# Branch projections as three-pass split products, and first inputs of four row-wise products split beside the stage ahead of them

## The reference

```
merged = gm[:, :, 0] * (o_nsa @ w_br_nsa[i]) + gm[:, :, 1] * (o_mla @ w_br_mla[i])
x = x + _rmsnorm(merged @ w_o[i], g_post_mix[i])
h = _rmsnorm(x, g_pre_ffn[i])
u = _causal_dwconv(h @ w_up[i], w_conv[i], b_conv[i])
a, v = u[..., :D_FF], u[..., D_FF:]
x = x + _rmsnorm((jax.nn.gelu(a) * v) @ w_down[i], g_post_ffn[i])
```

## Time and profile before

| | |
|---|---|
| median of 3 runs | 2354.74 us (2350.78 to 2355.29) |
| the profiled execution | 2355.66 us, span 2353.9 us |
| PE, DVE, ACT, POOL busy | 93%, 45%, 34%, 10% of the span |
| granted TensorE clock, mean | 0.95 |
| moved by DMA | 191.94 MB, 82 GB/s |

### The profile page before, as it was taken

The page is one execution under the profiler, slowest core; times in us unless marked ns, Lnnn a source line. Parts: engine busy times, 40 slices in busy tenths (PEclk is TensorE's granted clock), DMA queues, the critical chain, the costliest instruction groups (busy, mean ns, idle before and its releaser), DMA issues. The chain is left out here.

```text
span 2353.9 us, 26016 instructions
## 1 busy us (share of the span) xinstructions
PE 2178.9 (93%) x10269; PEld 1754.1 (75%) x10269; DVE 1048.0 (45%) x1829; ACT 808.5 (34%) x1467; POOL 227.4 (10%) x347
## 2 busy tenths in 40 slices
PE   6999989899999997999886899999999878999998
PEld 5886554678887874888775788788778657887887
DVE  4333662455554344222885433333442555333333
ACT  3154660343333233322012332322341664223222
POOL 8100000100000002000552100000110011000000
PEclk9999999999999998999676899999999988999999
DMA  5336311233332221322000133223243102232231
GB/s 133 86 107 96 44 36 54 89 99 90 107 91 90 96 101 45 107 90 90 18 1 1 63 107 97 100 90 100 80 134 125 54 1 75 96 108 90 90 108 72
DMA packets 162103, 191.94 MB, mean 82 GB/s; under 512 B 22866, under 2 KB 133757, under 8 KB 161981
## 3 DMA queue, kind: packets, MB, share of 16 engines
q1 hardware_dynamic: 157536, 176.15, 23.7%
q0 software_dynamic: 3904, 13.97, 3.2%
q10 hardware_dynamic: 541, 0.15, 0.0%
HBM read 182.91 MB, written 7.34 MB: 81 GB/s over the span
## 5 line engine op out<-in xcount | busy, mean ns | idle before, releaser
L1259 DVE TENSOR_TENSOR WHL<-raw,WHL 128x1024 fp32r<-128x1024 f32 x312 | 382.3, 1226 | 732.8 <-ACT WHL L808 732.6
L808 ACT ACTIVATE WHL<-raw 128x1024 fp32r<-128x1024 f32 x312 | 328.3, 1053 | 624.7 <-PE bank L1961 414.1
L1961 PE MATMUL bank<-WHL,HXh 128*128 128x512 f32 x1888 | 512.5, 394 | 18.1 <-DVE HXl L1267 12.3
L1860 PE MATMUL bank<-HXh,WHL 128*128 128x512 f32 x1248 | 494.6, 396 | 5.0 <-DVE BIG L1383 1.8
L1862 PE MATMUL bank<-HXh,WHL 128*128 128x512 f32 x1248 | 489.2, 392 | 0.0
L1961 PEld LDWEIGHTS bank<-WHL,HXh 128*128 128x128 f32 x1888 | 358.5, 190 | 95.8 <-issue 19.3
L1861 PE MATMUL bank<-HXl,WHL 128*128 128x512 f32 x1056 | 413.6, 392 | 0.0
L1860 PEld LDWEIGHTS bank<-HXh,WHL 128*128 128x128 f32 x1248 | 237.3, 190 | 55.2 <-issue 5.7
L1862 PEld LDWEIGHTS bank<-HXh,WHL 128*128 128x128 f32 x1248 | 236.9, 190 | 49.9
L1961 PE MATMUL bank<-WHL,HXl 128*128 128x512 f32 x880 | 273.2, 392 | 0.0
L1861 PEld LDWEIGHTS bank<-HXl,WHL 128*128 128x128 f32 x1056 | 200.3, 190 | 40.5
(11 more groups left out here) (292 smaller groups left out, 2521.0 us busy)
## 6 DMA issues: line engine op xcount, KB each, us to landing
raw<-in_mlp_w_up_dram SPq DMA_DIRECT2D x64, 512.0 KB, 4.6
raw<-in_mlp_w_down_dram SPq DMA_DIRECT2D x64, 512.0 KB, 4.3
raw<-in_w_up_dram SPq DMA_DIRECT2D x44, 512.0 KB, 4.9
raw<-in_a_w_in_dram SPq DMA_DIRECT2D x32, 512.0 KB, 4.3
raw<-in_w_in_dram SPq DMA_DIRECT2D x24, 512.0 KB, 4.8
raw<-in_w_down_dram SPq DMA_DIRECT2D x22, 512.0 KB, 4.1
raw<-in_w_kv_dram SPq DMA_DIRECT2D x16, 512.0 KB, 4.7
rel_dram<-GB POOLq DMA_DIRECT2D x1, 5120.0 KB, 54.5
```

Source lines behind the costliest of these rows:

```text
L808: return a.activation(dst, src, ACT.Copy, **k)
L1259: v.tensor_tensor(dst(1), src, dst(0).bitcast(F32), ALU.subtract).then_inc(w_lo, 1)
L1860: m.matmul(b[:, :], w[0][:, k, :], x[0][:, k, :], start=(k == 0), stop=False)
L1961: ins = m.matmul(bank[2 * tt + h][:, :], x, w[:, h * HALF:(h + 1) * HALF], start=(k == 0 and i == 0), stop=(k == nk - 1 and i == 2))
```

## The change

1. The branch weights are no longer in WHOLE: each slot is two units, split by ACT and DVE like other weights. The inputs are split too: high copies from HT to HX2l on ACT (`branch_high`), low parts in place of HT, as HXh, on DVE (`branch_low`). PE makes 24 split products a unit (`branch_product`), in eight banks, over b = 0 to 3 (half and branch) and j = 0, 1 (which two of the four k).
2. The first four inputs of w_o, down, down0 and down1 (EARLY) get tensors of their own, HX2h and HXl for w_o and HX2h alone for the others (`row_x`), and are split inside the stage ahead: on ACT by `rows_begin`, on DVE by `rows_split` with begin, which then returns. The stage's own call makes the rest.
3. The output of every row-wise product starts at bank 4 (`ybank`), so tiles 0 and 1 lie in banks 4 to 7. PE's wait for the whole stage ahead becomes one ahead of tile 2 at k = 0; for w_o the tiles go 2, 3, 0, 1 at k = 0, with a wait each.

The core of the diff:

```diff
-WHOLE = ("nsa_ck_w1", "nsa_cv_w1", "w_uq", "w_ukv", "br_nsa", "br_mla", "ple")
+WHOLE = ("nsa_ck_w1", "nsa_cv_w1", "w_uq", "w_ukv", "ple")
+EARLY = ("w_o", "down", "down0", "down1")
...
+        def ybank(tt, h):
+            return bank[(2 * tt + h + 4) % 8]
@@ ACT, attention_pairs @@
+                    if p == P_ALL:
+                        branch_high(0)
                     if p + 1 < p1:
                         exp_pair(p + 1)
...
+                    if p == P_ALL:
+                        split(branch_unit(0))
@@ ACT, after the attention @@
+            split(branch_unit(0, 1))
+            branch_high(4)
+            split(branch_unit(1))
+            for b in range(4):
+                split(branch_unit(b) + HL)
+                split(branch_unit(b) + HL + 1)
+                if b == 2:
+                    rows_begin(mergedT, "w_o", lambda k: (merged, k + 1))
             act.wait_ge(ps_full, GT["br"][0] + 16)
-            split(unit_at["w_o", 0])
@@ DVE, the loop over 16 groups @@
+                if f4 == 0:
+                    split(branch_unit(i // 4) + HL)
...
+                if f4 == 3:
+                    split(branch_unit(i // 4) + HL + 1)
+                if i == 11:
+                    rows_split("w_o", mergedT)
+            rows_split("w_o", mergedT, False)
@@ DVE, the up stage, after its waits for the group and for conv_act @@
+                    if j == NFF - 1 and s == 1:
+                        rows_split("down", uT)
@@ DVE, mlp, ahead of its wait for the relu @@
+                    if f == NFF2 - 1:
+                        rows_split(f"down{l}", uT)
@@ PE, split_rows @@
+                    if k == 0 and name == "w_o":
+                        pe.wait_ge(ps_free["vec"], GT["br"][2] + (14, 16, 10, 12)[tt])
+                    elif k == 0 and tt == 2 and name in EARLY:
+                        up = {"down": "up", "down0": "up0", "down1": "up1"}[name]
+                        pe.wait_ge(ps_free[GT[up][1]], GT[up][2] + (2 * NFF if up == "up" else NFF2))
@@ PE, branch_product @@
+                        m.matmul(dst[:, :], wh[:, k, cols_], HX2l[:, n, :], start=(j + k == 0), stop=False)
+                        m.matmul(dst[:, :], wh[:, k, cols_], HXh[:, n, :], start=False, stop=False)
+                        ins = m.matmul(dst[:, :], wl[:, k, cols_], HX2l[:, n, :], start=False, stop=(j == 1 and k == 1))
...
-            pe.wait_ge(merged, KD)
+            for b in range(4):
+                for j in range(2):
+                    branch_product(b, j)
```

More of the change, by code:

```diff
@@ L537, in ht0, with row_x @@
             return 8 * n
+        def ybank(tt, h):
+            return bank[(2 * tt + h + 4) % 8]
+        def row_x(name, k):
+            if name == "w_o" and k < 4:
+                return HX2h[:, k, :], HXl[:, k, :]
+            if name in EARLY and k < 4:
+                return HX2h[:, k, :], HX2h[:, 4 + k, :]
+            h, l = pair(name == "w_o")
+            return h[:, k % KD, :], l[:, k % KD, :]
         def pair(first_block):
@@ L831, in high @@
                         act.wait_ge(*unit_free[w + k - KD])
[L832 to L837, removed]
+                    copy(row_x(name, k)[0], x[:, k, :]).then_inc(x_hi, 1)
+                if name in EARLY:
+                    split(w + 2)
+                else:
+                    for k in range(4):
+                        high(k)
+                        if k == 1:
+                            split(w + 2)
                 for k in range(nk):
@@ L842, in rows_split, with rows_begin @@
                         split(w + k + HL)
+            def rows_begin(x, name, ready):
+                for k in range(4):
+                    act.wait_ge(*ready(k))
+                    copy(row_x(name, k)[0], x[:, k, :]).then_inc(x_hi, 1)
             def wait_group(name, i):
@@ L939, in turned_pair, with branch_high @@
                         copy(probT(p, x)[:, 512 * i:512 * (i + 1)], bank[4 + i][:, :]).then_inc(pt_act, 1)
+            def branch_high(k0):
+                for k in range(k0, k0 + 4):
+                    act.wait_ge(o_evac, k + 1)
+                    copy(HX2l[:, k, :], HT[:, k, :]).then_inc(br_hi, 1)
             def attention_pairs(p0, p1, per):
@@ L1076, in _ @@
                         split(unit_at["up", 2 * j + s] + HL)
+                    if j == NFF - 1 and s == 0:
+                        rows_begin(uT, "down", lambda k: (u_ready, k + 1))
                 act.wait_ge(conv_vec, 2 * j + 1)
@@ L1266, in low @@
                     vec.wait_ge(x_hi, x0[name] + k + 1)
[L1267 to L1273, removed]
+                    xh, xl = row_x(name, k)
+                    v.tensor_tensor(xl, x[:, k, :], xh.bitcast(F32), ALU.subtract).then_inc(x_lo, 1)
+                if begin:
+                    for k in range(4):
+                        low(k)
+                        if k == 1 and name not in EARLY:
+                            split(w + 2)
+                    if name in EARLY:
+                        return
+                else:
+                    split(w + 2)
                 for k in range(nk):
@@ L1550, in _, with branch_low @@
             attention_pairs(P_MLA, P_ALL, lambda p: lambda x: caus, lambda p: None)
+            def branch_low(k0):
+                for k in range(k0, k0 + 4):
+                    vec.wait_ge(br_hi, k + 1)
+                    v.tensor_tensor(HXh[:, k, :], HT[:, k, :], HX2l[:, k, :].bitcast(F32),
+                                    ALU.subtract).then_inc(br_lo, 1)
+            branch_low(0)
+            split(branch_unit(0))
+            split(branch_unit(0, 1))
+            branch_low(4)
+            split(branch_unit(1))
             for i in range(16):
@@ L1973, in split_rows @@
                     x_ready_for(k)
-                    for tt in range(TT):
+                    for tt in ((2, 3, 0, 1) if k == 0 and name == "w_o" else range(TT)):
                         ins = products(k, tt, *w)
```

75 lines of the change are left out of this document (43 added, 32 removed).

## The result

The changed kernel takes 2323.52 us in the median, the kernel before 2352.76 in the runs beside it: a ratio of 0.9872 (0.9853 to 0.9892), 30 us faster (25 to 35). The 30 us come from the ratio; the two medians lie 29.2 apart. One of the four executions of the changed kernel took 4337.55 us and is left out of the ratio; it is in the median, which is 2323.08 without it. The forecast was 2329.5, range 2324 to 2338: the direction is right, the time lies half a microsecond outside the range.

What follows compares the result with a forecast made beforehand. TensorE (PE), busy 93% of the span, was taken as the bound. Savings of 18.1 (branches to w_o's end), 3.1 (down) and 4.6 (down0, down1) made 25.8 us, giving 2329.5 us, range 2324 to 2338.

Steps and rivals of the forecast that it cites:

- The branches: Branch projection: 192 split products of 0.2267 us replace 64 of 0.853, 43.5 us instead of 55.2, 11.7 less.
- The wait and the low clock at w_o: Between branches and w_o: the 4.2 us wait goes, and 1.8 us of low clock behind it.
- The earlier start of 0.35: Start of the branches: PE finds first weight and inputs at 360.65 us at the latest, not 361.00.
- down: Start of down: 3.1 us saved, 1.5 of it clock, with two new stalls of 1.7 and 0.65 us left.
- down0 and down1: Ahead of each of these stages the 2.2 us wait and the issue beside it go: 2.3 us each, 4.6 together.
- Nothing behind it waits on a clock of its own: Behind w_o: residual and norm simply follow the last product, so its 18.1 us earlier end carries through.
- (a): Start of the branches: the first split comes late and the hole moves there, at most 6.0 us, 2335.5; chance 0.11.
- (b): down, down0, down1: early inputs bring nothing because another wait takes their place, 7.7 us back, 2337.2; chance 0.05.
- (c): Larger gain: branch products nearer 0.213 us, 2.6 less, and a stall kept out elsewhere, 2326; chance 0.07.
- (d): Branches: DVE becomes the bound, two MLA blocks at 3 us beyond, 2335; chance 0.03.
- (e): Branches: 192 weight loads of 0.19 us stand beside the products, 36 us on top, 2366, slower; chance 0.02.
- four passes for true FP32: Branches: a skill's rule leaving three of four passes, 41.4 us and 2 us more saved; the forecast followed the trace's 43.5.

Runs made afterwards that it cites:

- down_lows_first: The changed kernel with DVE's four low inputs of down made ahead of its wait for up's last group; 2322.90 us, ratio 0.9879.
- late_w_o: The changed kernel with PE made to wait ahead of w_o for its fifth low input; 2327.99 us, ratio 0.9906.
- early_only: The kernel before with early inputs for down, down0 and down1 and shifted banks, branches and w_o's start as before; 2340.84 us, ratio 0.9964.

## Why the prediction was right and wrong

**The terms.** The branches: forecast 43.5, measured 43.8, so 11.4 us less rather than 11.7; the pace of another stage's products was the right price. The wait and the low clock at w_o: 4.4 and 1.7, forecast 4.2 and 1.8. The earlier start of 0.35 can't be read, since the same code takes 354.7 or 361.0 us to get there. down 3.3 (3.1 forecast), with the first wait as foretold, 1.74, and the second smaller than the 0.65 foretold: 0.19 by the record, 0.5 by down's length against down_lows_first (120.41 and 119.93). down0 and down1 2.44 each (2.3). Sum 25.7 us, forecast 25.8 (25.45 without the earlier start). No wait of PE for a transfer shows in these stages.

**What failed** is that the sum put everything outside the touched stages at nothing: "Nothing behind it waits on a clock of its own: the residual and norm follow the last product", and 25.8 us came off the base with no term for the stretches behind. The terms measure 25.7 us, but the changed kernel is 29.2 and 29.4 us faster by the medians of its two comparisons, and 29.6 by the traces. In the traces the difference is 3.8 us in untouched stretches: norm and up 1.2, HGRN and h_out 1.4, down0's end to up1 1.3, the rest -0.1. For norm and up the runs show how: full clock came back 11.8 us behind the norm's first transposition in before and 9.5 in the changed kernel, and the stretch's length follows that return. So what stands behind w_o does hang on a clock, the one granted to TensorE.

Of the 6.0 us between forecast and measured time this is 3.4 (29.2 for 25.8). Another 2.0 is the base: the forecast started from 2354.74, and the kernel before took 2352.76 in the runs beside the changed one. The last 0.6 is the step from 2354.74 - 25.8 = 2328.9 up to 2329.5. The range was too narrow for either: "the three runs lie 4.5 us apart, so 2326 to 2333" stands on three runs, and the kernel before takes 2343 to 2355.6 over the later ones, with medians of 2349.2, 2349.3, 2350.8 and 2350.1 in four comparisons.

**What stays open** is how much of the 3.8 us the change always brings. norm and up was long in all five traces with the old branches or the old start of w_o (250.3 to 250.6), and short in six of the seven unpadded w_o stages that follow the new branches without a wait (249.2 to 249.3, and 249.8 in down_lows_first); but it was short in late_w_o, which has the wait. before's last three stretches took the short sum in one of two traces. HGRN and h_out range from 403.6 to 408.6 us over the unpadded kernels, whose code there is the same but for h_out's banks, so their 1.4 may be chance. Each interval of the gain, 25 to 35 and 24 to 34 us, just reaches 25.7.

**The rivals.** (a) did not come: PE got its first split unit in time by 0.16 us, where 0.1 was forecast. (b) did not: early_only is worth what its terms say. (c), a larger gain, was the direction, but not its mechanism: from one product's start to the next it is 0.227 us, not 0.213. (d) and (e) fell: PE loads 193 weights under 194 products in 43.5 us. The rule of the Trainium skill ("TensorE: Matmul & The Clock Gate", The mechanism) that loads overlap products only where row groups differ does not hold in the new stage either; the same section also lets a load run ahead into a background weight buffer, which the prediction did not weigh. The Trainium skill's four passes for true FP32 ("FP8 and Floating Point Precision", TensorE Precision Notes) would have put the branches at 41.4 us; they take 43.8.

## What to carry to other kernels

Price a new form of product by the pitch of the same form elsewhere in the trace, and look first for the hole between stages: splitting alone brought 10 us in its own stretches, and it took inputs made ahead to close the 4.4 us hole and save the 1.7 us of low clock behind it. Give the stages behind a change a term of their own where the granted clock falls ahead of them: here their length hung on when it came back, 1.2 us for norm and up. This kernel has a spread of its own (12 us of 2350) that three runs don't show; the range has to hold that spread of the base, not only the doubts in the sum. Compare traces stage by stage before a difference of a few microseconds is given a cause.

## What the runs showed of the hardware

The length of a stretch that starts at the low clock follows the moment at which full clock comes back for good. Over 16 traces norm and up take 249.1 us for a return 9.2 us behind its first transposition, and 250.6 for one at 12.5; norm and up1 183.8 for 9.2 and 185.3 for 12.4. The same code gave both, and 8 more products in each row-wise stage made up0's stretch 1.2 us shorter.

Waits of PE ahead of a row-wise stage that ran at full clock until then: 1.74 us never lowered the clock (11 traces), 2.2 did once in seven, 2.7 in the one case, 3.9 to 4.7 in all ten. Each fall behind such a wait cost 1.6 to 2.6 us in slow products on top of the wait.
